# Norms and layer starts of a four-layer hybrid trunk: squares added on VectorE, a sum moved, the router first, tiles begun together

## The reference

```python
for li in range(DEPTH):                       # DEPTH = 4
    sh1, sc1, g1, sh2, sc2, g2 = modulation(cond, w_mod[li], b_mod[li])
    h = x * (1 + sc1) + sh1
    out = mixer(h, ...)                       # gmlp, ssd, hgrn2, gmlp
    x = layer_norm(ALPHA * x + g1 * out, ln_g[li, 0], ln_b[li, 0])
    h = x * (1 + sc2) + sh2
    x = layer_norm(ALPHA * x + g2 * moe(h, ...), ln_g[li, 1], ln_b[li, 1])

def moe(h, w_router, b_router, w_gu, w_down):
    scores = sigmoid(h @ w_router)            # 16 experts in 4 groups
    # best group by its two best experts, then two experts of it, weighted
```

## Time and profile before

| what | value |
|---|---|
| median of 3 runs | 2985.69 us (2975.92 to 2989.59) |
| profiled execution, device time | 2981.99 us |
| its span, first to last instruction | 2980.2 us |
| mean granted TensorE clock | 0.914 |
| PE busy | 2643.8 us (89%) |
| DVE busy | 1462.1 us (49%) |
| POOL busy | 805.2 us (27%) |
| ACT busy | 745.8 us (25%) |
| DMA | 524.43 MB, mean 176 GB/s |

### The profile page before, as it was taken

The page is one execution under the profiler, slowest core; times in us unless marked ns, Lnnn a source line. Parts: engine busy times, 40 slices in busy tenths (PEclk is TensorE's granted clock), DMA queues, the critical chain, the costliest instruction groups (busy, mean ns, idle before and its releaser), DMA issues.

```text
span 2980.2 us, 30519 instructions
## 1 busy us (share of the span) xinstructions
PE 2643.8 (89%) x11934; PEld 1940.3 (65%) x11934; DVE 1462.1 (49%) x2288; ACT 745.8 (25%) x1255; POOL 805.2 (27%) x445
## 2 busy tenths in 40 slices
PE   5688989997997889899998877788999899989997
PEld 3687864445986678744457876676444599974444
DVE  7446443334549876533335578974333416650012
ACT  1132120002453442300014244423010233230111
POOL 3355300002443254000013558850000156500000
PEclk7789889998899999799998887897999999979999
DMA  7534639891330215388953321032989243428881
GB/s 269 170 113 126 201 111 353 323 348 62 105 111 29 71 57 170 113 311 323 350 186 119 128 74 34 20 123 97 350 323 361 100 130 112 141 100 281 297 298 47
DMA packets 291854, 524.43 MB, mean 176 GB/s; under 512 B 9472, under 2 KB 141056, under 8 KB 291328
## 3 DMA queue, kind: packets, MB, share of 16 engines
q1 hardware_dynamic: 288256, 519.33, 50.0%
q10 hardware_dynamic: 3456, 3.15, 0.3%
HBM read 517.73 MB, written 4.72 MB: 175 GB/s over the span
## 4 chain that ended last, share of the span: by engine, by line
PE 75%; DVE 12%; issue 4%; DMA 3%; ACT 3%; POOL 2%; SPq 0%; DVEq 0%; ACTq 0%
PE ps L1755 23%; PE ps L1770 11%; PE ps L1547 6%; PE ps L1549 6%; PE ps L1548 6%; PE ps L1581 3%; DVE macc L1840 3%; PE ps L1617 2%; POOL wlo L1479 2%; PE ps L1570 2%; PE ps L1571 1%; PE ps L1572 1%; DVE h L1870 1%; PE ps L1695 1%; PE ps L1609 1%
## 5 line engine op out<-in xcount | busy, mean ns | idle before, releaser
L1479 POOL TENSOR_TENSOR wlo<-ring,whi 128x1024 fp32r<-128x1024 f32 x202 | 529.0, 2634 | 1546.2 <-ACT whi L1346 1546.1
L1755 PE MATMUL ps<-ring,xg 128*128 128x512 f32 x1536 | 702.5, 602 | 0.0
L1755 PEld LDWEIGHTS ps<-ring,xg 128*128 128x128 f32 x1536 | 288.4, 193 | 326.2 <-issue 325.9
L1840 DVE SCALAR_TENSOR_TENSOR macc<-ring,cond_s,macc 128x1024 f32<-128x1024 f32 x322 | 436.9, 1417 | 10.5 <-DMA ring<-w_mod 10.5
L2051 DVE SCALAR_TENSOR_TENSOR hid<-ps,cws,sg 128x256 f32<-128x256 f32 x96 | 46.5, 484 | 667.9 <-ACT sg L1439 667.9
L1770 PE MATMUL ps<-ring,hidt 128*128 128x512 f32 x768 | 353.9, 604 | 2.3 <-ACT hidt L1413 2.3
L1547 PE MATMUL ps<-hh,whi 128*128 128x384 f32 x832 | 303.2, 364 | 28.2 <-POOL wlo L1479 18.3
L1346 ACT ACTIVATE whi<-ring 128x1024 fp32r<-128x1024 f32 x202 | 206.9, 1053 | 349.8 <-DMA ring<-gmlp_w_out 115.2
L1549 PE MATMUL ps<-hh,wlo 128*128 128x384 f32 x832 | 289.2, 348 | 0.0
L1548 PE MATMUL ps<-hl,whi 128*128 128x384 f32 x832 | 289.2, 348 | 0.0
L1770 PEld LDWEIGHTS ps<-ring,hidt 128*128 128x128 f32 x768 | 148.8, 194 | 190.3 <-issue 190.3
(11 more groups left out here) (327 smaller groups left out, 4185.1 us busy)
## 6 DMA issues: line engine op xcount, KB each, us to landing
ring<-moe_w_gu SPq DMA_DIRECT2D x192, 1024.0 KB, 7.8
ring<-w_mod SPq DMA_DIRECT2D x96, 1024.0 KB, 8.2
ring<-moe_w_down SPq DMA_DIRECT2D x96, 1024.0 KB, 5.7
ring<-gmlp_w_in SPq DMA_DIRECT2D x32, 1024.0 KB, 5.7
ring<-ssd_w_in SPq DMA_DIRECT2D x21, 1024.0 KB, 5.4
ring<-hgrn_w_in SPq DMA_DIRECT2D x20, 1024.0 KB, 5.2
ring<-gmlp_w_out SPq DMA_DIRECT2D x16, 1024.0 KB, 5.9
ring<-ssd_w_out SPq DMA_DIRECT2D x8, 1024.0 KB, 5.9
```

The costliest lines, as they stand in the source:

```text
L1479: pool.tensor_tensor(split_sub(wlo, s0), raw_sub(s0), split_sub(whi, s0).bitcast(F32), ALU.subtract).then_inc(S["lo_ready"], 1)
L1755: ins = pe.matmul(ps[:, s % 2, :], xg[:, w, k, :], whole(what, s, 4)[:, k % 4, :], start=(k == 0), stop=(k == KD - 1))
L1840: ins = dve.scalar_tensor_tensor(out=macc[:, v, :], in0=w[:, k, :], scalar=by, in1=macc[:, v, :], op0=ALU.mult, op1=ALU.add)
```

## The change

Five edits.

1. `variance`: VectorE adds the third and the fourth pair of square blocks to the second, and then the two blocks of that, and TensorE averages three blocks where it averaged eight.
2. The sum of group 6l + 6 moves from behind the last output tile to behind `variance(2l)`, ahead of the router; VectorE reads it after the norm. ScalarE applies a sigmoid to one column after the root of an even norm, so that the function's table is loaded there.
3. Routing: TensorE does the whole router before it transposes; then three groups of transposes, the ranks, the other three. VectorE takes two low halves after `gone` and four after the spread. The gather waits for three low halves, and from its fifth block on for all six.
4. `row_blocks`: at the start of a layer several tiles take each row block of h as it arrives, a tile with the number `behind` that many blocks later. Layer 1: the time-step tile and the first two full tiles (0, 0, 1 behind). Layer 2: four query tiles (0, 0, 1, 2 behind). Layer 3: two pairs of value halves (0, 1 behind).
5. Two semaphores that nothing waited for are gone.

```diff
@@ variance, mod_sum
-                for k in range(KD):
-                    pe.wait_ge(S["sq_ready"], 4 * q + k // 2 + 1)
-                    ins = pe.matmul(bank(5), mean_d[:, :], sq[:, k, :], start=(k == 0), stop=(k == KD - 1))
+                for k in range(3):
+                    if k == 0:
+                        pe.wait_ge(S["sq_ready"], 4 * q + 1)
+                    elif k == 2:
+                        pe.wait_ge(S["sq_added"], 3 * q + 3)
+                    ins = pe.matmul(bank(5), mean_d[:, :], sq[:, k, :], start=(k == 0), stop=(k == 2))
                 ins.then_inc(S["var_done"], 1)
...
                 variance(2 * l)
+                if l + 1 < DEPTH:
+                    mod_sum(6 * l + 6)
                 experts(l)
...
-            if l % 3 == 2:
-                done = {7: 6 * l + 6}
-            else:
-                done = {3: 6 * l + 5, 7: 6 * l + 6} if l + 1 < DEPTH else {7: 6 * l + 5}
-            return [done[m]] if m in done else []
+            return [6 * l + 5] if l % 3 < 2 and m == (3 if l + 1 < DEPTH else 7) else []
@@ layer_norm on ScalarE
                 act.activation(std[:, :], bank(5), ACT.Sqrt, bias=eps[:, 0:1]).then_inc(S["std_ready"], 1)
+                if q % 2 == 0:
+                    act.activation(table[:, :], eps[:, :], ACT.Sigmoid)
@@ layer_norm on VectorE
+                for j in (2, 3):
+                    dve.wait_ge(S["sq_ready"], 4 * q + j + 1)
+                    if j == 3:
+                        dve.wait_ge(S["sq_added"], 3 * q + 1)
+                    dve.tensor_tensor(sq[:, 2:4, :], sq[:, 2:4, :], sq[:, 2 * j:2 * j + 2, :], ALU.add).then_inc(S["sq_added"], 1)
+                dve.wait_ge(S["sq_added"], 3 * q + 2)
+                dve.tensor_tensor(sq[:, 2, :], sq[:, 2, :], sq[:, 3, :], ALU.add).then_inc(S["sq_added"], 1)
@@ experts on TensorE
-                    if k == 4:
-                        to_tokens(0)
-                to_tokens(1)
+                to_tokens(0)
...
                 ins.then_inc(S["rank_done"], 1)
-
-                pe.wait_ge(S["tlo_ready"], 2 * NT * (l + 1))
+                to_tokens(1)
+
+                pe.wait_ge(S["tlo_ready"], 2 * NT * l + NT)
                 pe.wait_ge(S["spread_ready"], NT * (l + 1))
                 for k in range(KD):
+                    if k == 4:
+                        pe.wait_ge(S["tlo_ready"], 2 * NT * (l + 1))
@@ route on VectorE
-                for i in range(NT, 2 * NT):
+                for i in range(2):
                     tokens_low(l, i)
...
                     dve.tensor_scalar(spread[:, t, :], iota[:, :], slot[:, t:t + 1], None, ALU.is_equal).then_inc(S["spread_ready"], 1)
+                for i in range(2, 2 * NT):
+                    tokens_low(l, i)
@@ starts of layers
+            def row_blocks(q, *tiles):
+                for step in range(KD + tiles[-1][0]):
+                    if step < KD:
+                        pe.wait_ge(S["hl_ready"], 8 * q + step + 1)
+                    for behind, block, subs in tiles:
+                        if 0 <= step - behind < KD:
+                            ins = block(step - behind)
+                            if step - behind == KD - 1:
+                                ins.then_inc(S["sub_done"], subs)
@@ pe_ssd (dt_block: the nine matmuls of a row block of the time-step tile)
+            first = [(0, dt_block, 2)]
+            for j in range(2):
+                pe.wait_ge(S["lo_ready"], nth[sb((l, "xs"), j)] + 1)
+                claim(j, "stage_ready", j + 1)
+                first.append((j, full_block(sb((l, "xs"), j), bank(j)), 1))
+            row_blocks(l, *first)
@@ pe_hgrn
+                    if part == "q" and j < 4:
+                        first.append((max(0, j - 1), full_block(s, bank(j)), 1))
+                        if j == 3:
+                            row_blocks(l, *first)
+                    else:
+                        full(s, bank(j % 4), hh, hl)
@@ gmlp
+                    if l and c == 0:
+                        first = token_block(s, [ps[:, t, 0:256] for t in range(NT)])
+                    elif l and c == 1:
+                        row_blocks(l, (0, first, 2), (1, token_block(s, [ps[:, 3 + t, 0:256] for t in range(NT)]), 2))
```

More of the change, by code:

```diff
@@ L624, in pe_ssd @@
                 pe.wait_ge(S["lo_ready"], nth[s] + 1)
-                if j == 0:
-                    for b in range(4):
-                        claim(b, "stage_ready", b + 1)
-                else:
-                    claim(j % 4, "stage_ready", j + 1) if j >= 4 else None
-                full(s, bank(j % 4), hh, hl)
+                if j >= 2:
+                    claim(j % 4, "stage_ready", j + 1)
+                    full(s, bank(j % 4), hh, hl)
                 if j == 1:
@@ L1054, in pe_hgrn @@
                     claim(j % 4, name, j + 1)
-                    full(s, bank(j % 4), hh, hl, arrives=("hl_ready", 8 * l) if part == "q" and j == 0 else None)
+                    if part == "q" and j < 4:
[3 more added lines that the diff above has]
+                    else:
+                        full(s, bank(j % 4), hh, hl)
                     if part == "f" and j == 2 * MOD_GROUP:
@@ L1471, in _ @@
         def _(pool):
-            chain = Chain(pool, S["pool_step"])
             fed = [0]
@@ L1573, in by_token, with full_block, block, token_block @@
                 ins.then_inc(S["sub_done"], 2)
+            def row_blocks(q, *tiles):
[7 more added lines that the diff above has]
+                                ins.then_inc(S["sub_done"], subs)
+            def full_block(s0, out):
+                def block(k):
+                    w = slice(k * P, (k + 1) * P)
+                    return product(out, whi[:, nth[s0] % SPL, w], wlo[:, nth[s0] % SPL, w], hh[:, k, :], hl[:, k, :], k == 0, k == KD - 1)
+                return block
+            def token_block(s0, outs):
+                pair = lambda w, k: w[:, nth[s0] % SPL:nth[s0] % SPL + 2, k * P:(k + 1) * P]
+                outs = [o.rearrange("p (a n) -> p a n", a=2) for o in outs]
+                def block(k):
+                    for t in range(NT):
+                        pe.matmul(outs[t], hh[:, k, toks(t)], pair(whi, k), start=(k == 0), stop=False)
+                        pe.matmul(outs[t], hl[:, k, toks(t)], pair(whi, k), start=False, stop=False)
+                        ins = pe.matmul(outs[t], hh[:, k, toks(t)], pair(wlo, k), start=False, stop=(k == KD - 1))
+                    return ins
+                return block
             def mod_sum(group):
@@ L2029, in experts @@
                 last_of = lambda s: s in mods and mods[s] % MOD_GROUP == MOD_GROUP - 1
-                for i in range(NT):
-                    tokens_low(l, i)
                 route(l)
@@ L2096, in _ @@
                 layer_norm(2 * l)
+                if more:
+                    mod_take(6 * l + 6)
                 experts(l)
```

36 lines of the change are left out of this document (17 added, 19 removed).

## The result

| | before | after |
|---|---|---|
| median of 6 runs, us | 2984.39 | 2963.39 |
| profiled execution, its time | 2981.99 | 2952.87 |
| its span | 2980.2 | 2951.1 |
| mean granted clock | 0.914 | 0.916 |

The changed kernel takes 0.9922 of the time before, 95% interval 0.9904 to 0.9939: 21.0 us by the medians, 29.1 by the two profiled spans.

The account below looks back on a forecast made before the run. TensorE was taken as the bound, with a serial ladder across engines in norms and routing. Norms 20.7 plus layer starts 4.5 made 25.2 us off the profiled 2981.99, so 2956.8; the forecast was 2958, range 2941 to 2971 us.

Parts of the forecast that it names:

- the squares: All eight norms: adding squares on VectorE shortens the way to the squares' sum; 7.6 us won.
- the sum's new place: Modulation sum ahead of the router: overhangs TensorE's 4.64 us wait at 1.2 GHz; router 2.0 us late in three layers, -6.0.
- each even norm: Squares added on VectorE in the four even norms: 1.6 us won in each, ends 1.4 and 2.1.
- each odd one: Squares added on VectorE in the four odd norms: 0.3 us won in each, ends 0 and 0.7.
- layer 3's start: Two pairs of value halves together: third pair's weights wait for pair 0's slot; 2.9 us lost, bounds 1.1 and 3.5.
- the adds end at 4.5, 5.4 and 5.95: Norms: us from the subtraction's start to VectorE's adds' ends, from 0.89 per add and 0.5 for the last.
- the squares' sum ending 6.7 to 7.4 us after the subtraction's start: Norms, sign in the profile after: last matmul done at 6.7 us at 2.4 GHz or 7.4 at 1.2 GHz.
- The wait for pair 0's slot: Layer 3's start: TensorE stands still 4.8 us until the third pair's weights arrive at 23.8, 1.1 us later than before.
- Layer 1's start: Time-step tile mixed with full tiles, clock staying low: acs done at 36.7 us against 35.6; 1.1 us lost.
- the rival with the clock risen: Layer 1's start at full clock: acs read near 24.5 us instead of 35.6, 11 us more, 2946; chance 0.15.
- Layer 2's start: Four query tiles share the row blocks, clock rises: eighth tile ends at 36.2 us instead of 44.75; 8.5 us won.
- the router's term: Router ahead of transposes ends 2.64 us earlier, way to gather grows from 7.8 to 9.1; 1.3 a layer, 5.2 won.

Follow-up runs that it names:

- u3: The changed kernel with the starts of layers 1 and 3 put back as before the change; ratio 0.9899 to before, 28.4 us below it.
- b3: Changed kernel with three-piece sum, old layer 3 start, gather banks swapped, layer 1 mixing 128-column time-step matmuls with one full tile; ratio 0.9846 to before.
- v5: The changed kernel with time-step matmuls of 128 columns instead of 64, the first 64 unused; ratio 0.9903 to before, 30.6 us below it.
- u4: The changed kernel with layer 2's start as before, one query tile on the row blocks; two executions count, 2967.60 and 2971.33 us.
- v2: The changed kernel with the gather taking banks 2 and 3 first; ratio 0.9921 to before, 25.2 us below it.

## Why the prediction was right, and where not

The time was right, 2958 for 2963, and mostly by its own mechanisms: each edit moved what it was said to move, and all but the odd norms in the direction that was said. The terms as measured add up to 20.9 us where 25.2 were forecast. There is some luck in it: the squares came out 4.5 us below the forecast and the sum's new place 2.1 above it, which partly cancel, and that the terms of one pair of traces meet the medians' 21.0 to a tenth is chance, since the interval of the ratio allows 18 to 29 us.

The sum started from the profiled execution; taken from the median, 2985.69, the same 25.2 us would have given 2960.5. The sizes of three terms were off, and two of them lie outside the bounds set for them: each even norm won 1.1 (bounds 1.4 and 2.1), each odd one lost 0.35 in the mean (0 and 0.7 won), and layer 3's start lost 3.7 (1.1 and 3.5).

- *Squares added on VectorE*, 7.6 forecast, 3.1 found. The step that failed is "the adds end at 4.5, 5.4 and 5.95, and the last matmul's two passes take 0.65 us at 2.4 GHz or 1.3 at 1.2 GHz". The adds end at 4.6, 5.6 and 6.2. The 0.89 was a mean of four subtractions that overlap; one alone takes 0.96, and so does an add, and each add waits for the one before, so that they start 1.07 us apart (715.32 and 716.39 in the chain). The two passes take 1.65 us at 1.2 GHz (the row at 1206.06 above), not 1.3, and 0.92 at 2.4 GHz (layer 0), not 0.65. So 7.95 and not 7.4, and the sign "the squares' sum ending 6.7 to 7.4 us after the subtraction's start" failed in six norms (7.9) and held in two (7.2). Three of the odd norms lose 0.54 each instead of winning 0.3; the last wins 0.2. "I expect its clock to be low more often" was right, in six norms of eight.
- *The sum in its new place*, -6.0 forecast, -3.9 found. "7.0 us" at 1.2 GHz was right (6.6 to 6.9), but it starts right behind the squares, before the root, so 1.8 us hang over and not 2.0 to 2.3; and in layer 0 the clock rose within it and 0.2 us were lost. The cause is tested: with the squares on TensorE, and with the sum in pieces, the 3.9 us are gone.
- *Layer 3's start*, -2.9 forecast, -3.7 found. The wait for pair 0's slot was forecast at 4.8 us and is 4.54, but the third pair started 1.6 us later than before, not 1.1, and the low clock behind it cost 2.1 instead of 1.8. u3 gives the 3.7 back.

Layer 1's start came out as worked out (37.2 for 36.7), and the rival with the clock risen was wrong for this kernel: 31 us without a gap, at 0.50. The Trainium skill (TensorE: Matmul & The Clock Gate, "Why this matters for your kernels") says that a TensorE kept busy without a break goes to its full clock; here the trace disagrees, in this start and in b3's 25 us. v5, which changes nothing but the width of the time-step matmuls, shows that the width kept it down in this start; b3 shows that the wide ones alone don't raise it when only one full tile is mixed in. As a rival it had acs read at 24.5 us, 11 before the old 35.6; in v5 it is read at 27.5, 8.1 ahead of before and 9.7 ahead of the changed kernel.

Layer 2's start won 7.6 of 8.5: the eighth tile ends at 37.2 where 36.2 was forecast, and nearly all of that is there when the first four end, at 19.3 for 18.4. The wait for the first tile's slot was the one reckoned with; ScalarE's half of the next chunk then waited 3.7 us for a load and TensorE less than 1 us. u4 confirms the size.

Of the router's term the way to the gather was right to the tenth (9.1 us, four times), and v2 shows that the three low halves behind the spread are its cause; the router itself ends 2.45 us earlier and not 2.64, so the term is 4.8 and not 5.2. No run takes the router's order back, so these 2.45 us are read from the traces alone.

What the prediction lacked is the spread of the clock. TensorE waits 2.73 us for the first u tile of layer 3 in the changed kernel and in v2 alike; windows behind that wait, first of the changed kernel, then of v2:

```profile
2446.30:2449.30 3.00, 2.94 (x17) 2.94 (x18) 2.96 (x3) 2.60 (x4) 3.00 (x2) 1.00 0.74 249
```

```profile
2453.90:2456.90 3.00, 3.00 (x10) 3.00 (x10) 2.96 (x3) 2.25 (x3) 3.00 (x2) 0.50 0.63 218
```

The same work behind the same wait, once at 1.00 and once at 0.50. Such a place was worth 1.6 to 3.0 us in the ledger, and every layer has some; most of the 8.2 us between the pair of traces and the sum of the terms is made of them. It stays open why the clock falls at one of them and not at another.

## What to carry to other kernels

A tile mixed into a critical one delays it by all that is mixed in: share the arriving blocks among tiles only where none of them is waited for first, and where the slots that they free aren't wanted one by one. Work moved into a wait has to fit at the clock that the work ahead of it leaves; cut it into pieces that fit several waits. Ledger a change place by place from two traces, look at the granted clock wherever two kernels differ at a place that they share, and don't count such a difference as gain.

## What the runs showed of the hardware

A matmul with 64 columns and one with 128 both started every 0.213 us at 1.2 GHz. Nine of 64 columns taking turns with six of 384 kept the granted clock at 0.50 for 31 us; nine of 128 with the same six had it at 1.00 ten microseconds after the start; nine of 128 with three of 384 kept it at 0.50 for 25 us. The first of these three mixes was seen in seven kernels, the other two in one each. An f32 add of two SBUF operands of 128x768 took 0.96 us on VectorE, the subtraction with one operand in PSUM 0.95. A table load takes 1.28 us on ScalarE, and the sigmoid after it began at once.
